# The last layer's mixer as one sequence of 25 weight units over a ring of three PSUM banks, with attention heads among the gate units and low halves made by GpSimd

## What is computed

```
h = rms_norm_2(stream, mix_norm_g)              # 272 x 1024
proj = h @ w_in                                 # conv value and gate 2x1024, q 8x128, k 2x128, v 2x128,
                                                # q_idx 8x64, k_idx 64, w_idx 8, gates 2x1024
q, k, q_idx, k_idx = rope(...)                  # x1*cos - x2*sin, x2*cos + x1*sin
y_a = silu(layer_norm(depthwise_conv(a * sigmoid(gate), width 31))) @ conv_pw_out
score = sum_h w_idx[h] * relu(q_idx[h] . k_idx) # causal; meta keys get a bonus
keep the 68 best keys of each query             # top_k = 272 // 4
y_b = softmax(q . k, over the kept keys) @ v @ attn_w_o   # 8 query heads over 2 key heads
g_a, g_b = sigmoid(gates)
stream = stream + (g_a * y_a + g_b * y_b) @ w_merge_out
```

## Time and profile before

| what | us |
|---|---|
| median of 3 runs | 1181.6 (1181.05 to 1183.11) |
| the profiled execution | 1182.05 |
| its span | 1179.5 |
| PE busy | 1126.3 (95%) |
| DVE busy | 796.3 (68%) |
| ACT busy | 571.7 (48%) |
| POOL busy | 101.0 (9%) |
| share of PE on the chain that ended last | 84% |

### The profile page before, as it was taken

One profiled execution on the slowest core, in us unless ns is written; L12 is line 12 of the kernel. 1 busy time (PEld: TensorE's weight loads), 2 busy tenths in 40 slices (PEclk: granted clock), 3 DMA queues, 4 the chain that ended last, 5 costly groups with the idle time before them and its releaser, 6 DMA issues.

```text
span 1179.5 us, 22345 instructions
## 1 busy us (share of the span) xinstructions
PE 1126.3 (95%) x8886; PEld 1087.0 (92%) x8886; DVE 796.3 (68%) x1255; ACT 571.7 (48%) x828; POOL 101.0 (9%) x110
## 2 busy tenths in 40 slices
PE   7997999999999999999998999897999998999998
PEld 7996999999999999999998899796778988999997
DVE  6766555555567766565554698999868657788743
ACT  4666544435445555444444543332455546556542
POOL 1332020002031203000000000100100000000000
PEclk9999999999999999999999899999998999999999
DMA  8744256647673444555457345244112444555460
GB/s 256 205 126 143 73 179 184 208 133 233 205 249 118 134 143 144 172 184 181 137 186 245 91 146 159 88 144 143 57 52 95 156 144 142 178 167 172 140 199 36
DMA packets 187924, 181.33 MB, mean 154 GB/s; under 512 B 17935, under 2 KB 186268, under 8 KB 187851
## 3 DMA queue, kind: packets, MB, share of 16 engines
q1 hardware_dynamic: 187323, 178.22, 48.0%
q0 software_dynamic: 528, 2.10, 0.6%
HBM read 179.25 MB, written 1.05 MB: 153 GB/s over the span
## 4 chain that ended last, share of the span: by engine, by line
PE 84%; DVE 8%; ACT 4%; POOL 2%; issue 2%; DMA 0%; SPq 0%; ACTq 0%; DVEq 0%; POOLq 0%
PE ps L518 25%; PE ps L519 24%; PE ps L520 24%; DVE work L2481 2%; DVE w_lo L370 2%; POOL work L444 2%; PE ps L674 2%; ACT w_hi L356 1%; PE ps L2139 1%; PE ps L427 1%; PE ps L1976 1%; PE ps L919 1%; PE ps L665 1%; PE ps L1983 1%; PE ps L1780 0%
## 5 line engine op out<-in xcount | busy, mean ns | idle before, releaser
L518 PE MATMUL ps<-u_hi,w_hi 128*128 128x256 f32 (+2 forms) x1864 | 534.6, 287 | 16.1 <-DVE u_lo L487 6.9
L519 PE MATMUL ps<-u_lo,w_hi 128*128 128x256 f32 (+2 forms) x1864 | 530.3, 284 | 0.0
L520 PE MATMUL ps<-u_hi,w_lo 128*128 128x256 f32 (+2 forms) x1864 | 529.5, 284 | 0.0
L370 DVE TENSOR_TENSOR w_lo<-raw,w_hi 128x2048 fp32r<-128x2048 f32 (+3 forms) x182 | 382.6, 2111 | 158.3 <-ACT w_hi L356 157.8
L518 PEld LDWEIGHTS ps<-u_hi,w_hi 128*128 128x128 f32 x1864 | 356.1, 191 | 18.9 <-issue 14.1
L520 PEld LDWEIGHTS ps<-u_hi,w_lo 128*128 128x128 f32 x1864 | 356.2, 191 | 0.0
L519 PEld LDWEIGHTS ps<-u_lo,w_hi 128*128 128x128 f32 x1864 | 355.7, 191 | 0.5
L356 ACT ACTIVATE w_hi<-raw 128x2048 fp32r<-128x2048 f32 (+3 forms) x182 | 316.0, 1753 | 42.6 <-PE ps L520 32.0
L519 PE MATMUL ps<-a_lo,w_hi 128*128 128x256 f32 x528 | 148.0, 280 | 0.0
L520 PE MATMUL ps<-a_hi,w_lo 128*128 128x256 f32 x528 | 147.6, 280 | 0.0
L518 PE MATMUL ps<-a_hi,w_hi 128*128 128x256 f32 x528 | 147.0, 278 | 0.1
(11 more groups left out here) (307 smaller groups left out, 1295.7 us busy)
## 6 DMA issues: line engine op xcount, KB each, us to landing
raw<-in_w_in SPq DMA_DIRECT2D x24, 1024.0 KB, 5.3
raw<-in_w_gate SPq DMA_DIRECT2D x22, 1024.0 KB, 5.3
raw<-in_w_up SPq DMA_DIRECT2D x22, 1024.0 KB, 5.3
raw<-in_ffn_up SPq DMA_DIRECT2D x22, 1024.0 KB, 5.1
raw<-in_w_down SPq DMA_DIRECT2D x16, 768.0 KB, 4.8
raw<-in_od_w_qkv SPq DMA_DIRECT2D x12, 1024.0 KB, 5.2
raw<-in_w_down SPq DMA_DIRECT2D x16, 640.0 KB, 4.8
raw<-in_ev_w_in SPq DMA_DIRECT2D x7, 1024.0 KB, 10.3
```

The lines of the kernel that those rows point to most:

```text
L370: nc.vector.tensor_tensor(w_lo[t % RING][:, 0:n], raw[t % RAW][:, 0:n], w_hi[t % RING][:, 0:n].bitcast(F32), ALU.subtract).then_inc(lo_don ...
L518: nc.tensor.matmul(out_ap, a_h, b_h, start=start and n == 0, stop=False)
L519: nc.tensor.matmul(out_ap, a_h, b_l, start=False, stop=False)
L520: mm = nc.tensor.matmul(out_ap, a_l, b_h, start=False, stop=stop and n == len(pairs) - 1)
```

## The change

The five phases become one, `ph_mix`, with its 25 units in a new order: convolution gate and value pairs mixed with index units, k, q, then v, then the eight gate units. The sequence is numbered in groups x of three products (400 in all); everything else is hung on such numbers, on every engine (`ROT_AT`, `COS_AT`, `SIN_AT`, `IDX_SLOTS`, `TOP_SLOTS`, `PICK_AT`, `COLS_AT`, `META_SLOTS`, `DSA_SLOTS`, `SUM_SLOTS`, `conv_due`).

- A tile of 128 output columns has one of three PSUM banks in turn and is freed by itself (`mix_read`).
- Banks 3 and 4 hold index scores and head scores, 5 and 6 the rotations, later the turned probabilities and the outputs; 7 holds the taps' sums.
- Taps accumulate in PSUM (bank 7), read `cin` of SBUF, cover the 256 real tokens only, and the last one writes `work`. The two needed meta tokens get their convolution as a product and a reduction (`first_tokens`).
- The first rope step (times cos) reads the projection's bank; ACT copies it for the rotation. Ropes of q cover 258 columns, of q_idx 256.
- `k_d` and `ki_half` hold their keys twice, so that each query block's keys lie in one piece; `ki_half` is zero in the other head's rows, so q is no longer copied into padding.
- Heads stand every ten groups from 276. Values are feature-major: V is stationary, the turned probabilities move; probabilities are scaled by ACT before they are turned. The meta keys' part is one product of 32 rows with `v_meta`, made from a doubled copy of u (`u_twice`, GpSimd).
- The two meta queries of all eight heads go as one small head (`META_SLOTS`).
- The gate units are copied raw, the sigmoids done in two pieces (`gates_open`).
- GpSimd makes the low halves of 25 units, from the mixer's third unit to the projection's second, in four pieces each.
- Three of the four channel sums move into the sequence; the layer norm's halves no longer wait for the projection, which reads `o2_hi` and `o2_lo`.

```
+    POOL_LO = range(ph_mix.u0 + AHEAD, ph_wo.u0 + AHEAD)
+    def split_lo_pool(t):
+        n, parts = widths[t], 4
+        nc.gpsimd.wait_ge(hi_done, t + 1)
+        nc.gpsimd.wait_ge(lo_done, t)
+        for at in range(0, n, n // parts):
+            cols = slice(at, at + n // parts)
+            a = nc.gpsimd.tensor_tensor(w_lo[t % RING][:, cols], raw[t % RAW][:, cols], w_hi[t % RING][:, cols].bitcast(F32),
+                                        ALU.subtract)
+        a.then_inc(lo_done, 1)
...
+    MIX_UNITS = [("cg", 0), ("cv", 0), ("ki", 0), ("qi", 0), ("qi", 1), ("cg", 1), ("cv", 1), ("kp", 0), ("q", 0),
+                 ("cg", 2), ("cv", 2), ("q", 1), ("q", 2), ("cg", 3), ("cv", 3), ("q", 3), ("v", 0)] + \
+        [("g", n) for n in range(2 * D // UC)]
...
+        ROT_AT.setdefault(start + n + 6, []).append(r)
+        COS_AT.setdefault(start + (n if n == KT else (t + 1) * KT) + 3, []).append(T)
+        SIN_AT.setdefault(start + n + 7, []).append(r)
...
+    IDX_SLOTS = [90 + 6 * n for n in range(IH)]
+    TOP_SLOTS = [140 + 11 * r for r in range(TOP_ROUNDS + 1)]
+    PICK_AT, COLS_AT = 238, 246
+    META_SLOTS = {266: "scores", 280: "turn", 288: "values"}
+    DSA_SLOTS = [276 + 10 * n for n in range(10)]
+    SUM_SLOTS = [376, 382, 388]
...
+    def conv_due(x):
+        if 36 <= x < 136 or 236 <= x < 272:
+            return x % 4 == 0
+        if 136 <= x < 236:
+            return x % 8 == 0
+        return x >= 272 and x % 2 == 0
...
+        def meta_queries():
+            act.wait_ge(sem("rope_done"), ROPE_FIRST + len(ROPES))
+            nc.scalar.activation(q_first[:].rearrange("p (h t) -> p h t", t=2), q_d[:, :, 0:2], ACT.Copy).then_inc(sem("q_first"), 1)
...
+        def dsa_values(n):
+            g = n // 4
+            dh = slice(g * DH, (g + 1) * DH)
+            pe.wait_ge(sem("dsa_ptc"), n + 1)
...
+            own = pt4[:, n % 2, :]
+            for b, tokens in enumerate(((0,), (0, 1))):
+                o = ps[:, 6, b * P:(b + 1) * P]
+                for m, v in enumerate(tokens):
+                    at = (b + m) * P
+                    nc.tensor.matmul(o, v_d[:, v, dh], own[:, at:at + P], start=m == 0, stop=False)
+                mm = nc.tensor.matmul(o, v_meta[:, b, dh], own[0:2 * META, 3 * P:], start=False, stop=True)
+            mm.then_inc(sem("dsa_o"), 1)
...
+            if name == "scores":
+                pe.wait_ge(sem("q_first"), 1)
...
+                for t in range(2):
+                    tile = 2 * j + t
+                    own, ends = ps[:, 7, t * T1:(t + 1) * T1], work[:, tile, 2:NF]
+                    wait(dve, sem("conv_tap"), (j * taps + w - 1) * 2 + t - 1)
+                    nc.vector.scalar_tensor_tensor(out=ends if w == taps else own, in0=cin[:, tile, w + META:w + T2],
+                                                   scalar=conv_w[:, tile, w:w + 1], in1=ends if w == 1 else own,
                                                    op0=ALU.mult, op1=ALU.add).then_inc(sem("conv_tap"), 1)
```

More of the change, by code:

```diff
@@ L96, with __init__ @@
 class Phase:
-    def __init__(self, plan, units, body, group=1, dmas=None, peel=0, pairs=4, widths=None, first=0):
+    def __init__(self, plan, units, body, group=1, dmas=None, peel=0, pairs=4, widths=None, first=0, paired=True):
         self.u0, self.units, self.body, self.group = plan["units"], units, body, group
@@ L110, in __init__ @@
             plan["loads"][(self.u0 + n) % RAW] += 16 * d
-        for n in range(units // group):
+        for n in range(units // group if paired else 0):
             plan["used"][n % self.groups % pairs] += 1
@@ new lines, in build, with mix_tile, mix_done, mix_released @@
+    MIX_END = at
+    mix_read = [sem(f"mix_read{n}") for n in range(3)]
+    def mix_tile(kind, n, t):
+        return next(T for T, (u, tt, _) in enumerate(MIX_TILES) if MIX_UNITS[u] == (kind, n) and tt == t)
+    def mix_done(eng, T):
+        u, _, last = MIX_TILES[T]
+        if last:
+            eng.wait_ge(unit_done, ph_mix.unit(0, u) + 1)
+        else:
+            eng.wait_ge(sem("mix_half"), sum(not q for _, _, q in MIX_TILES[:T + 1]))
+    def mix_released(eng, T):
+        eng.wait_ge(mix_read[T % 3], T // 3 + 1)
@@ new lines, in mix_bank, with add_rope @@
+    def mix_bank(T, n):
+        return ps[:, T % 3, 0:n]
+    ROPES, ROPE_OF = [], {}
+    ROPE_FIRST = 3
+    def add_rope(tile, raw_ap, width, x0, dim, into):
+        ROPE_OF[tile] = len(ROPES)
+        ROPES.append((raw_ap, width, c(f"rot{dim}"), c(f"cos{dim}")[:, x0:x0 + width], c(f"sin{dim}")[:, x0:x0 + width], into))
+    everywhere = slice(0, P)
+    ki_rows = [slice(64 * e, 64 * e + 64) for e in range(2)]
+    add_rope(mix_tile("ki", 0, 0), ki[:], T2, 0, 64,
+             [(ki_half[r, e, P:], r, slice(0, T2)) for e, r in enumerate(ki_rows)] +
+             [(ki_half[r, e, 0:P], r, slice(META, META + P)) for e, r in enumerate(ki_rows)])
@@ L1602, in first_tap @@
                                          bias=gains[:, bias:bias + 1])
             a.then_inc(sem("first_tap"), 1)
-        for i, k in ph_conv.steps(act):
-            split_hi(ph_conv, i, k)
-            if k and k % 2 == 0:
-                first_tap(k // 2 - 1)
-            if k % 2 == 0:
-                p = ph_conv.pair(k)
-                act.wait_ge(unit_done, ph_conv.unit(i, k) + 1)
-                wait(act, pair_read[ph_conv.pair(k + 1)], ph_conv.used_before(i, k + 1))
-                nc.scalar.activation(sg4[:, (k // 2) % 2], pair_ap(p, T2), ACT.Sigmoid).then_inc(pair_read[p], 1)
@@ L1647, in _ @@
-        for i, k in ph_gate.steps(act):
-            split_hi(ph_gate, i, k)
-            p = ph_gate.pair(k)
-            act.wait_ge(unit_done, ph_gate.unit(i, k) + 1)
-            nc.scalar.activation(paired(gates)[:, k], pair_ap(p, NF), ACT.Sigmoid).then_inc(pair_read[p], 1)
-        act.preload_act_table_set("natural_log_exp_and_others")
-        def gate_b(n):
-            if n % 2 and n // 2 < ph_gate_b.units:
-                split_hi(ph_gate_b, 0, n // 2)
-            elif n and n % 2 == 0:
-                gate_b_out(n // 2 - 1)
```

946 lines of the change are left out of this document (484 added, 462 removed).

## The result

| | before | after |
|---|---|---|
| median (range), us | 1181.3 (1180.8 to 1183.1) | 1150.25 (1148.6 to 1150.9) |
| runs | 4 | 4 |
| profiled execution, us | 1182.05 | 1148.63 |
| its span | 1179.5 | 1146.8 |
| granted clock, mean | 0.978 | 0.981 |

The account below looks back on a forecast made before the run. PE bounds the first half; from 785 us it also waits for DVE, with slow clock behind and a serial end. Gains 35.3 - 7.0 - 1.7 - 1.5 = 25.1; 1182.05 - 25.1 - 0.45 = 1156.5 us, range 1142 to 1170.

Parts of the forecast that it names:

- 30.3 - 7.0 - 1.7 - 1.5: Mixer up to the projection: 30.3 us gained, less 7.0 PE wait, 1.7 slow clock and 1.5 among heads.
- stall: PE waits before the q_first scores at group 266 for DVE's pick and ropes: 7 us, plus 1.7 slow clock.
- heads: Each head's PE work falls from 4.33 to 3.5 us, 6.8 us less over eight heads.
- slots: Ten groups and one head, 7.1 us; the scores-to-probabilities chain fits barely, 1.5 us put for it.
- terms for DVE behind group 238: Pick 5.6, three tap pairs 2.4, six rope steps 2.2, columns 2.6: DVE through some 13.3 us later.
- those from 136 to 238: DVE's rounds with taps 20, 13 tap pairs 10.7, ropes and gatings 8: 38.5 of PE's 40.5 us.
- Low halves on GpSimd: 25 low-half subtractions leave DVE for GpSimd, four pieces each, 5.2 us a unit, hidden behind PE.
- The projection's stretch: From the output projection's start to the pointwise products: 28.8 us instead of 33.8, gain 5.0.
- No stall: Rival: DVE ahead of its slots, few collisions, values at 0.21: 1142 to 1148 us; chance 0.11.
- The heads' chain: Rival: each head slot waits 1.5 to 2 us, GpSimd's lock adds to the pick: 1165 to 1175 us; chance 0.15.
- GpSimd as the bound: Rival: low halves taking over 9 us a unit lose time; at 13 about 1219 us; chance 0.08.
- Late banks: Rival: PSUM banks freed late as evictions and first rope steps queue behind rounds: about 1172 us; chance 0.06.

Follow-up runs that it names:

- a_skip: Changed kernel with GpSimd leaving out the low halves of mixer units 17 and 18, the only ones made during DVE's pick: 1142.1 us.
- a_pick256: Changed kernel with the pick moved from group 238 to 256, behind the last ropes' sums, and the two-token columns from 246 to 300: 1143.1 us.
- a_pick_meta: a_pick256 with the small head's maxima and reciprocal right behind the pick and its scaling on ACT at 271: 1144.9 us.
- a_dve_lo: Changed kernel with all low halves of the mixer back on DVE, six groups behind each unit's start: 1163.8 us.
- a_taps_sbuf: Changed kernel with the taps accumulating in SBUF (work) as before the change, GpSimd still making the low halves: 1179.2 us.

## Why the prediction came out as it did

**Right, and in part by luck.** From the mixer's start to the projection the sum was 30.3 - 7.0 - 1.7 - 1.5 = 20.1 us, and 20.1 were measured. Its terms were not all as good as that. The *stall* was put at 7.0 us with 1.7 of slow clock; it took 8.9 in two waits, 2.6 of slow clock behind the second and some 0.8 between the two (eight products 0.21 apart), 12.3 against 8.7. The *heads* paid for it: from the values' first product to the end of the next head's scores and turns PE takes 805.15 to 808.32, 3.2 us, where 3.5 were put, 2.6 us over eight heads; and the *slots*, put at 1.5, cost a single wait of 0.6. So an error of 3.6 us and two that make 3.5 cancel: that the stretch came out at 20.1 to the tenth is luck; the same mixer took 209.9 to 212.4 us in four profiles.

**The mechanism of the stall** was named in its place (the scores of `q_first`, behind DVE's last rope sums), in its cause (the pick, colliding with GpSimd, in a DVE with no slack) and nearly in size: a_skip bears out the collision, a_pick256 the place in the order, and a_pick_meta the lack of slack. Missed was that the wait splits: the cosine step behind the pick holds a bank of the ring first. The prediction had counted what is queued behind PE's wait and behind DVE's ropes, not which bank the ropes free. Its terms for DVE behind group 238 (5.6, 2.4, 2.2, 2.6) also add up to 12.8 us and not to 13.3, and those from 136 to 238 (20, 10.7, 8) to 38.7 and not to 38.5, with 13 tap pairs at 0.8 being 10.4; none of these slips moves the forecast by more than 0.5.

**Low halves on GpSimd** were put at 5.2 us a unit from the fold's 1.30 of the earlier trace rows; they take 5.0, 1.25 a piece, 5.6 where they collide. Units are started in time: one wait for `w_lo` of 0.7 us. That they pay is shown by a_dve_lo (13.5 us), and that this needs the taps in PSUM by a_taps_sbuf (25 us more in the mixer). **The projection's stretch**: 28.8 forecast, 29.1 measured.

**The rivals.** No stall: excluded, 8.9 us. The heads' chain: excluded at 0.6 us of waits. GpSimd as the bound: its pieces would have had to take 2.2 us and more. Late banks: one case of it happened, the rope's, for 4.4 us, but as part of the stall.

**Where it was off** is the unstated term: that all that the change doesn't touch stays as it is. It didn't, by 6.4 us ahead of the mixer and 1.5 behind, and this is 7.9 us of gain beside a forecast of 25.1; 25.1 and 7.9 are 33.0, and the two spans differ by 32.7. (By the medians it is 31.1: the profiled execution of the changed kernel was the fastest of its four, 1.6 us below their median.) 5.1 of the 7.9 come with the allocation, 1.5 with the third down projection's pace, 1.3 with the clock ahead of the mixer. The wider constants stood in the diff. No row that was read from the profile of before told what they do to the products' pace.

## What to carry to other kernels

Before work is moved to GpSimd, list DVE's instructions beside it by where their operands lie: one operand in PSUM kept 224 taps at 482 ns, where SBUF made them 751 and the mixer 25 us longer. Within a full engine, put first what the bound engine needs next, and the long collided step behind it: that alone was worth 7 us here. And where a change moves tiles, compare the untouched stretches of both profiles first: some 5 of these 31 us came with 160 bytes of allocation, and 96 bytes more took them away again. Where executions differ for such reasons, read a change's own stretch beside the whole time.

## What the runs showed of the hardware

- GpSimd subtracts 512 fp32 columns into fp32r in 1.25 us, four of them in 5.02, about the same as its addition in fp32 (1.30).
- A DVE instruction with two fp32 inputs in SBUF takes 486 ns without GpSimd's pieces beside it and 745 to 751 with them; with one input in PSUM it takes 482 beside them.
- DVE's scalar operations on one SBUF tensor of fp32 collide with GpSimd as those on two do: 0.29 us became 0.94 and 1.33, and an operation on 128x2 went from 0.17 (a_skip) to 1.07.
- A 256-column fp32r product has two paces at the full clock, 0.113 and 0.118 us from start to start (the kernel before shows 0.117 in one phase), mostly kept for a whole phase. The first two down projections were at the short one in each of nine profiled kernels where their moving tile stood 64 bytes past a multiple of 256, and at the long one in each of three where it stood at 160 or 192; but the third, at the same addresses, was at the long one in two of the nine, and with u moved as well, two executions of one kernel differed in it. What chooses is open.
- With a gap of 4.4 us PE's granted clock fell to a half: the eight products behind it stood 0.21 us apart, and after a second gap of 4.5 us, 1.7 us later, it stayed there for 5.9 us. In a_pick256 gaps of 1.4 and 3.0 us in the same place cost no clock (granted 1.00).
